# Loads of the first stage on one queue, twelve vector tiles instead of eight, the first latent pair over six banks, and two pool tiles worked block by block

## Time and profile before

| what | value |
|---|---|
| runs shown | 2049.58, 2051.52, 2054.91 us, median 2051.52 |
| profiled execution | 2055.45 us, of which the span from first to last instruction is 2053.6 |
| TensorE busy | 1880.6 us, 92% of the span |
| DVE / ACT / POOL busy | 1199.4 / 401.1 / 117.9 us |
| mean granted TensorE clock | 0.959 |
| DMA traffic | 316.08 MB, 154 GB/s on average |
| first big tile of the z stage starts | 161.58 us |
| first pool tiles | from 1357.99 us |

### The profile page before, as it was taken

One profiled execution on the slowest core, in us unless ns is written; L12 is line 12 of the kernel. 1 busy time (PEld: TensorE's weight loads), 2 busy tenths in 40 slices (PEclk: granted clock), 3 DMA queues, 4 the chain that ended last, 5 costly groups with the idle time before them and its releaser, 6 DMA issues.

```text
span 2053.6 us, 32904 instructions
## 1 busy us (share of the span) xinstructions
PE 1880.6 (92%) x13314; PEld 1721.4 (84%) x13314; DVE 1199.4 (58%) x1589; ACT 401.1 (20%) x884; POOL 117.9 (6%) x93
## 2 busy tenths in 40 slices
PE   4889999999999989998888899958999999999995
PEld 2239999999999977776777779958999999999995
DVE  3738667766976654552455544377777544574444
ACT  2121000000000112331455543440000000121111
POOL 2000000000600000000000011200000000001110
PEclk9999999999999999998799998979999999999997
DMA  9765545555654431204333254214545332552222
GB/s 385 293 228 182 203 185 191 201 210 210 223 213 186 170 114 52 78 22 154 99 115 116 90 193 142 92 41 166 185 185 194 117 121 103 179 186 82 82 82 87
DMA packets 86251, 316.08 MB, mean 154 GB/s; under 512 B 12200, under 2 KB 20568, under 8 KB 60464
## 3 DMA queue, kind: packets, MB, share of 16 engines
q1 hardware_dynamic: 63200, 229.31, 31.0%
q10 hardware_dynamic: 21200, 76.48, 10.3%
q0 software_dynamic: 1792, 9.49, 1.2%
HBM read 282.56 MB, written 32.69 MB: 154 GB/s over the span
## 4 chain that ended last, share of the span: by engine, by line
PE 69%; DVE 13%; DMA 8%; issue 5%; ACT 5%; SPq 0%; DVEq 0%; ACTq 0%; POOL 0%; POOLq 0%
PE banks L719 68%; DMA w_adr<-in_w_ada_dve 4%; DMA w_raw<-in_w_pin 3%; DVE banks L1633 2%; ACT pxd L1410 1%; DVE std L1881 1%; DVE w_hi L1592 1%; DMA d_raw<-pool_d_scratch 1%; DVE rstd L1572 1%; DVE x L2082 1%; DVE pt_lo L1815 0%; ACT px L1328 0%; DVE w_hi L1865 0%; DVE stage L2048 0%; DMA w_raw<-in_w_out 0%
## 5 line engine op out<-in xcount | busy, mean ns | idle before, releaser
L719 PE MATMUL banks<-h_hi,w_hi 128*128 128x272 f32 x3968 | 830.7, 295 | 57.5 <-DVE w_lo L1593 20.1
L719 PE MATMUL banks<-h_lo,w_hi 128*128 128x272 f32 x3712 | 776.8, 291 | 0.0
L719 PE MATMUL banks<-h_hi,w_lo 128*128 128x272 f32 x3456 | 721.7, 291 | 0.0
L719 PEld LDWEIGHTS banks<-h_hi,w_hi 128*128 128x128 f32 x3968 | 634.0, 193 | 68.6 <-issue 46.2
L719 PEld LDWEIGHTS banks<-h_lo,w_hi 128*128 128x128 f32 x3712 | 594.8, 192 | 0.0
L719 PEld LDWEIGHTS banks<-h_hi,w_lo 128*128 128x128 f32 x3456 | 546.2, 191 | 0.0
L1633 DVE CUSTOM_DVE_ANT_0 banks<-w_adr,cond_b 128x2048 f32<-128x2048 f32 x144 | 335.2, 2328 | 29.2 <-DMA w_adr<-in_w_ada_dve 26.6
L1592 DVE CAST w_hi<-w_raw 128x2048 fp32r<-128x2048 f32 x100 | 124.5, 1245 | 223.2 <-PE banks L719 171.2
L1593 DVE TENSOR_TENSOR w_lo<-w_raw,w_hi 128x2048 fp32r<-128x2048 f32 x100 | 246.9, 2469 | 3.5
L1265 ACT ACTIVATE stage<-banks 128x544 f32<-128x544 f32 x46 | 28.9, 628 | 496.3 <-PE banks L719 496.3
L1973 DVE TENSOR_TENSOR x<-x,stage 128x544 f32 (+1 forms) x32 | 24.0, 749 | 169.4 <-ACT stage L1492 169.4
(11 more groups left out here) (308 smaller groups left out, 1614.6 us busy)
## 6 DMA issues: line engine op xcount, KB each, us to landing
w_adr<-in_w_ada_dve ACTq DMA_DIRECT2D x46, 1024.0 KB, 5.1
w_raw<-in_w_z SPq DMA_DIRECT2D x32, 1024.0 KB, 6.9
w_raw<-in_w_pin SPq DMA_DIRECT2D x32, 1024.0 KB, 5.8
w_more<-in_w_ada_pe SPq DMA_DIRECT2D x19, 1024.0 KB, 7.1
w_adr<-in_w_ada_dve SPq DMA_DIRECT2D x18, 1024.0 KB, 4.9
w_raw<-in_w_gate SPq DMA_DIRECT2D x16, 1024.0 KB, 6.7
w_raw<-in_w_out SPq DMA_DIRECT2D x32, 512.0 KB, 3.9
w_raw<-in_w_pout SPq DMA_DIRECT2D x16, 1024.0 KB, 4.9
```

The costliest lines, as they stand in the source:

```text
L719: return pe.matmul(out, lhsT, rhs, start=start, stop=stop)
```

## The change

- `ADA_PE` goes from 24 to 20 and `ADA_P0` from 8 to 12. All loads of the first stage except the small constants are issued by SP, pieces and DVE tiles alternating, x in two halves between them. The DVE tiles get four buffers, two of them under `h_hi`. Squares are summed after pieces 1 and 2.
- ACT instead of DVE takes the turned chunks with the bias (four small operations per chunk); `h_hi` is written after chunks 2, 3 and 4.
- The first pair's items go to bank pairs 2, 4, 6 by `item_bank`, with fewer waits (`FIRST_EV`). The kpe product goes to banks 0 and 1 after the second item.
- The split of `G_PIN + 1` stands before `row_var(1)`, TensorE works both tiles per block k, the loop's splits are one tile further ahead, and the weight loads of a pass are those of the next pass. `silu(cond_b)` stands before the last pass of `gated`. In the groups the splits stand behind the four outputs, for the group after next.

The core of the diff:

```diff
-ADA_PE = 24
-ADA_P0 = 8
+ADA_PE = 20
+ADA_P0 = 12
-PE_MOD = (KT + 8, KT + 12, 0, 4, 8, 12)
+PE_MOD = (KT + 12, 0, 4, 8, 12)
+        def item_bank(t, k):
+            pair = 2 if t else (2, 4, 6, 2, 2, 4, 6, 6, 2)[k]
+            return pair + (k - I_K if k in (I_K, I_K + 1) else k - I_V if k in (I_V, I_V + 1) else 0)
+        FIRST_EV = (0, 0, 0, 1, 1, 3, 3, 3, 4)
...
+            def load_scale(a):
+                if a >= 4:
+                    sp.wait_ge(adr_used, a - 3)
+                sp.dma_start(scale_slots[a % 4], w_ada_dve[a]).then_inc(scale_in[a % 4], 16)
+            load_piece(0)
+            load_scale(0)
+            load_piece(1)
+            load_scale(1)
+            load_scale(2)
+            sp.dma_start(x[:, 0:KT // 2], xT[:, 0:KT // 2]).then_inc(x_in, 16)
+            load_piece(2)
+            load_scale(3)
+            sp.dma_start(x[:, KT // 2:KT], xT[:, KT // 2:KT]).then_inc(x_rest_in, 16)
+            load_piece(3)
+            load_scale(4)
+            load_scale(5)
+            for g in range(4, 10):
+                load_piece(g)
+                load_scale(g + 2)
+            for g in range(10, ADA_PE):
+                load_piece(g)
...
+            for s in range(2):
+                load_w(w_pin[s], (G_PIN + s) % 2, G_PIN - G_KPE + s)
             with sp.Fori(0, KT // 2) as t:
                 for s in range(2):
-                    load_w(tile_of(wp2, s, t), (G_PIN + s) % 2, 2 * t + G_PIN - G_KPE + s)
+                    load_w(tile_of(wp2, s, t + 1), (G_PIN + s) % 2, 2 * t + G_PIN + 2 - G_KPE + s)
                 for s in range(2):
                     sp.wait_ge(adr_used, 2 * t + (ADA_P0 + ADA_P1 + s))
                     sp.dma_start(w_adr[:, 1], tile_of(wd2, s, t + (ADA_P0 + ADA_P1) // 2)).then_inc(adr_in[s], 16)
...
-                big_tile((G_PIN + s) % 2, KT)
+            for k in range(KT):
+                pe.wait_ge(h_ready, KT + k + 3)
+                for s in range(2):
+                    m = tile_products((G_PIN + s) % 2, k, k == 0, k == KT - 1)
+                    if k == KT - 1:
+                        m.then_inc(mm_done, 1)
...
             for c in range(CHUNKS):
                 act.wait_ge(mm_done, 4 * c + 4)
-                if c:
-                    act.wait_ge(ada_turned, c)
                 act.activation(stage[0:2, 1, 0:512], PS[0:2, 2, :], ACT.Copy).then_inc(ada_row, 1)
+                act.wait_ge(ada_turned, c + 1)
+                for q in range(4):
+                    m = PE_MOD[c] + q
+                    ins = act.activation(mod[:, :, m], PS[:, 3, 2 * (4 * c + q):2 * (4 * c + q) + 2], ACT.Identity,
+                                         bias=bada_t[:, m:m + 1])
+                ins.then_inc(mod_ready, 1)
...
-                if c >= 3:
-                    upper_h0(c - 3)
-            upper_h0(3)
+                if c == 2:
+                    upper_h0(0)
+                if c >= 2:
+                    upper_h0(c - 1)
...
             fold_scale(1)
+            split(G_PIN + 1)
             row_var(1)
...
-                    split(G_PIN + 1, dve_t2, t)
+                    split(G_PIN + 2, dve_t2, t)
...
-                    split(G_PIN + 2, dve_t2, t)
+                    split(G_PIN + 3, dve_t2, t)
...
             for g in range(4):
-                split(G_GRP + g + 1)
                 group_out(4 * g)
                 if g < 3:
                     lower_d(g + 1)
                 for n in range(1, 4):
                     group_out(4 * g + n)
+                if g < 3:
+                    split(G_GRP + g + 2)
```

More of the change, by code:

```diff
@@ L317, in program @@
         ring_in = [sem(f"ring_in{i}") for i in range(RING)]
-        scale_in = [sem(f"scale_in{s}") for s in range(2)]
+        scale_in = [sem(f"scale_in{s}") for s in range(4)]
         adr_in = [sem(f"adr_in{s}") for s in range(2)]
@@ L822, in _ @@
             big_tile((G_GATE + GT - 1) % 2)
-            pe.wait_ge(mq_var, 2)
-            for a in range(2):
-                m = small(PS[:, 6 + a, 0:HALF], swap_t[:], kpe[:, a * HALF:(a + 1) * HALF], True, True)
-            m.then_inc(kp_swap, 1)
-            for s in range(2):
-                pe.wait_ge(acc_free[s], turn_of(G_OUT + (G_OUT + s) % 2))
+            pe.wait_ge(acc_free[1], turn_of(G_OUT + (G_OUT + 1) % 2))
             pe.wait_ge(mq_var, 2)
             pe.wait_ge(mq_norm, 1)
-            pe.wait_ge(masks_ready, 1)
             halves = [slice(0, HALF), slice(HALF, R)]
@@ L836, in item @@
                 e0 = ITEMS * t
+                b = item_bank(t, k)
+                if t == 0 and FIRST_EV[k]:
+                    pe.wait_ge(ml_ev, FIRST_EV[k])
                 if k in (I_Q, I_Q + 1, I_ROPE):
@@ L920, in _ @@
                 item(0, k)
+                if k == I_Q + 1:
+                    pe.wait_ge(acc_free[0], turn_of(G_OUT + G_OUT % 2))
+                    for a in range(2):
+                        m = small(PS[:, a, 0:HALF], swap_t[:], kpe[:, a * HALF:(a + 1) * HALF], True, True)
+                    m.then_inc(kp_swap, 1)
             for w in range(ML_UNITS + LAG + 1):
@@ L1321, in _ @@
                 item_hi(0, k)
+                if k == I_Q + 1:
+                    act.wait_ge(mq_norm, 2)
+                    act.dma_start(ckv_out.rearrange("t p r -> p t r"), ckT[:]).then_inc(latent_out, 16)
+                if k == I_K + 1:
+                    act.wait_ge(kp_done, 1)
+                    act.activation(kpe_hi[:], kpe[:], ACT.Copy).then_inc(kp_hi, 1)
+                    act.dma_start(kpe_out, kpe[0:DQK, :]).then_inc(latent_out, 16)
             for w in range(ML_UNITS + LAG + 1):
@@ L1501, in _ @@
                 gated(t, G_O2, 1, 2 * KT, halves=True)
+            act.wait_ge(condb_in, 32)
+            act.activation(cond_b[:], cond_b[:], ACT.Silu).then_inc(condb_ready, 1)
             with act.Fori(KT // 2 - 1, KT // 2) as t:
@@ L1505, in _ @@
             affine1()
-            act.wait_ge(condb_in, 32)
-            act.activation(cond_b[:], cond_b[:], ACT.Silu).then_inc(condb_ready, 1)
             act.wait_ge(pad_zero, 1)
@@ L1804, in _ @@
                 item_out(0, k)
+                if k == I_Q + 1:
+                    dve.wait_ge(kp_swap, 1)
+                    dve.tensor_tensor(rows(qpr[:]), PS[:, 0:2, 0:HALF], rows(sin_t[:]), ALU.mult)
+                    vchain(dve, dve.tensor_tensor(kpe[:], kpe[:], cos_t[:], ALU.mult))
+                    vchain(dve, dve.tensor_tensor(kpe[:], kpe[:], qpr[:], ALU.add))
+                    dve.memset(lam_in[:, 0, 0:1], 0.0).then_inc(kp_done, 1)
+                if k == I_SWAP:
+                    dve.wait_ge(kp_hi, 1)
+                    dve.tensor_tensor(kpe_lo[:], kpe[:], kpe_hi[:].bitcast(F32), ALU.subtract).then_inc(kp_lo, 1)
             for w in range(ML_UNITS + LAG + 1):
```

163 lines of the change are left out of this document (71 added, 92 removed).

## The result

The changed kernel takes 1995.26 us in the median of 4 runs (1993.56 to 1997.15), the one before 2052.55 us beside it: ratio 0.9722, 95% interval 0.9705 to 0.9739, 57.3 us less. The forecast was 1992 us. The profiled execution took 1995.63 us, 1993.8 of them span, where the profiled one before had a span of 2053.6: 59.8 us less to explain.

What follows compares the result with a forecast made beforehand. TensorE, busy 92% of the span, was taken as the bound; -21.2 - 9.7 - 17.5 - 13.0 + 1.0 = -60.4 us from a median of 2051.5 us gave 1991, rounded up to 1992 us, range 1982 to 2011.

Steps and rivals of the forecast that it cites:

- Part 1: First stage: four pieces go and four DVE tiles come; z stage starts at 140.4 instead of 161.58 us, -21.2 us.
- rival (a): First stage: SP's one queue is the limit at 330 GB/s; 14 us less gain, 2006 us; chance 0.13.
- The landings by 417 GB/s: First stage: loads land at 2.51 us per MiB; DVE tile 4 at 43.9 us, piece 10 at 79.0.
- the square sums: First stage: TensorE's eight blocks of square sums come behind 38 us, from 39.5 to 47.5 us.
- Part 2: First latent pair: with six banks, scores start at 772.4 instead of 782.1 us, -9.7 us.
- The upper bound: First latent pair: the most to be gained is -11 us, from 8.7 of waits, 1.7 of slow second item and 0.9.
- Part 3: Pool stage: two first tiles by block with early split give -17.5 us, the loop another -13.0 us.
- the 1 us for `silu(cond_b)`: Before the pool tiles: the moved silu pushes the last eviction of `gated`, and the variance, about 1 us.
- rival (b): Pool loop stays held by modulation loads and `w_adr`, or block-wise stage runs mostly at 1.2 GHz; 2006 us; chance 0.15.
- Rival (d): Pool loop: TensorE does not return to 2.4 GHz after the block-wise stage; all 30 tiles low gives 2353 us; chance 0.01.
- Part 4: Groups: TensorE's wait goes from 2.91 to about 4.4 us, +1.5; later splits give back 0.5; +1.0 in the sum.
- the later splits: Groups: splits out of the way of outputs and `lower_d` give back the small waits, -0.5 us.

Runs made afterwards that it cites:

- e7: Changed kernel with the twelve VectorE tiles of stage one loaded by GpSimd's queue again, pieces alone on SyncE's; 2000.0 us, ratio 0.9741.
- e8: Changed kernel with the split of kpe's weights ahead of `h_lo` 4 to 7 instead of behind them; 1990.1 us, ratio 0.9691.
- e4: Changed kernel keeping SyncE's new load order and the silu's place, but splits put back and first two pool tiles one after the other; 2037.6 us, ratio 0.9933.
- e9: Changed kernel with the pool loop's first modulation tile issued ahead of the next pass's two weights, early split kept; 2017.8 us, ratio 0.9833.
- e11: Changed kernel with the last pool pass taken out of the loop and the second group's split behind `lower_d(0)`; 1993.0 us, ratio 0.9707.
- e3: Kernel before with only the pool-stage and group changes applied; 2025.8 us, ratio 0.9860.
- e2: Kernel before with only the first-latent-pair change applied (six banks, kpe swap moved, outputs stored later); 2040.4 us, ratio 0.9940.
- e1: Kernel before with only the first-stage change applied (12 VectorE and 20 TensorE pieces, everything on SyncE's queue); 2036.4 us, ratio 0.9914.
- e5: Changed kernel with the first two pool tiles one after the other on TensorE, second tile still split early; 1999.7 us, ratio 0.9733.
- e10: Changed kernel with one silu of a single element on ScalarE ahead of the pool loop; 1994.8 us, ratio 0.9716.

## Why the prediction was right

**The sum.** -60.4 us forecast, -59.8 measured between the two profiled executions. The forecast of 1992 us is 3.3 below the median of 1995.3, nearly all of it from where the sum was anchored: the profiled execution of before lay 3.9 us above its median, the one of after 0.4 above its own. The terms missed by more than the sum did, in both directions (+3.2, -1.9, -0.5, +1.2, and -1.3 in a stretch outside them), so that the sum came so close is in part luck; that each part gave what it did is not.

**Part 1, -21.2 forecast, -18.0 measured.** The mechanism held: rival (a), a queue limited to 330 GB/s, is out (427 GB/s), and e7 shows what the one queue is for, order and not rate. The landings by 417 GB/s were good to 2 us: VectorE's fifth tile at 45.68 instead of 43.9, its tiles done at 90.80 instead of 88.8, the first quarter of the kpe tile at 115.06 instead of 113.7. That quarter began 1.4 us late, and the lower clock behind the stop ahead of it (116 to 120 us at 0.57), 1.5 us by e8, was not in the sum. (The stop itself, put at some 2 us, was 3.63.) And the last blocks of h were done at 138.7 instead of 136.4, with four small operations for lambda, 0.8 us, between them and the z tile's split, which I had left out. One sign failed: the square sums were to come behind 38 us, in eight blocks from 39.5 to 47.5. The first eight ran from 31.42, at the lower clock (2.0 us a block against 1.1), the other eight from 45.5 to 53.1. TensorE then took the pieces back to back and had caught up with the loads at 81 us, so nothing was lost by it: VectorE set the time.

**Part 2, -9.7 forecast, -11.6 measured.** The upper bound was 11. The waits of the earlier trace rows went as said. The miss is in the sum of the work: 3.9, 3.9, 1.1, 3.9, 7.1, 1.2, 7.1 and 1.9 are lengths of rows, 30.1 us, and each row overlaps the next by some 0.2 us. From start to start the same work is 28.3 us. The prediction says "allowing for overlaps" but took nothing off for them.

**Part 3, -30.5 forecast (17.5 and 13.0), -31.0 measured from the first block on.** The third tile started at 1356.92 us; the forecast's 1388.6, moved by the 31.0 us that the stage began earlier (1357.99, 1327.02 after), is 1357.6, or 1356.6 without the 1 us for `silu(cond_b)`, which falls ahead of the first block: TensorE's wait there for POOL's `ssq` was 5.17 us instead of 3.97, which fits that 1 us. So the early part gave some 18 us and the loop 13.0. The loop ran at 24.05 us a pass without a wait of TensorE. VectorE's pass, put at 21.5 us, fits with room (3.5 + 0.3 us of a pass it waits for TensorE), its wait for `w_adr` was 3.0 us in all, so rival (b) did not come. Rival (d) did not either: the granted clock is 1.00 from 1365 us on. What the prediction did not see is how narrow the way is: it gave the loop's 13 us to the order of SyncE's loads and counted the early split only for the first tiles, and e4 and e9 show that the loop needs both.

**Part 4, +1.0 forecast, +2.2 measured.** The wait was 4.37 as said (4.4). The half microsecond to be given back by the later splits came too (0.6). Left out was the lower clock behind the stop, 1.5 us in the first group (0.79 us for a pair that takes 0.49). It isn't the greater length of the stop that brings it: e11 has the 2.91 us of the kernel before and the slow pair all the same.

**A reading that could mislead.** Between the first scores and the first block of the pool tiles nothing of weight was edited, yet the fourteen traces here took between 570.4 us (e7) and 579.2 (e3) for it; the changed kernel's is 574.5, with a granted clock of 0.76 to 0.95 in the stretches from 940 to 1190 us. The start of the z stage moves too where nothing ahead of it was edited: 161.58 us in the kernel before, 158.63 in e2, 160.00 in e3, and with the new first stage 143.5 in the changed kernel and 144.6 in e1. So the first stage's gain is 14 to 18 us, depending on the pair of traces; e1's median says 17.0. A single pair of traces can't tell a part's gain to better than that if the stretch lies between; the medians of e1 to e3 could.

## What to carry to other kernels

When an in-order queue of loads feeds an engine, write down for each load which release it waits for and which use it serves, over a whole pass: a load must not stand behind a wait that this pass's own work ends. Moving one load forward helps only if the release it waits for moves forward too; otherwise the wait goes to the load behind it. And count a stop of TensorE at more than its length: behind the stop of 3.6 us the lower clock cost 1.5 more (e8), behind the one of 3.0 it cost 1.8 more (e5).

## What the runs showed of the hardware

- One queue of plain loads, most of 1 MiB, moved 427 GB/s over 72 us; two queues moved 416 in the same stretch (e7).
- With `silu(cond_b)` moved away from the loop's entry, ScalarE loaded tables of activation functions in each pass of the loop: 30 loads of 1.28 us, gone with one element of silu ahead of the loop (ACT 443.3 to 406.6 us). The Trainium skill, "ScalarE: Activation LUTs", section What ACT_TABLE_LOAD costs, gives about 1283 ns for the load itself, and the trace agrees; that the loads come back in each pass for what stands ahead of the loop is shown by e10.
- Behind stops of 3.63, 2.73 and 2.34 us TensorE was granted its lower level (1.2 GHz) for part of the next microseconds, seen as 0.57 to 0.66 of full speed in the 4 us stretches above. The length of a stop alone does not tell what comes behind it. Behind 2.91 us ahead of the first group the first pair took 0.49 us in the kernel before and 0.80 in e11, both after over 100 us at 1.00. Behind 2.73 us ahead of the last quarter of the kpe tile it took 0.75 us in the changed kernel and 0.52 in e8, where the lower level came about 1.5 us later. No rule comes out of these rows, only what each stop cost.
